# Mixer of a hybrid streaming encoder layer: gate row products ahead of the small root on GpSimd, statistics and shift ahead of taps on VectorE, attention's high parts first on ScalarE

## The reference

```
mod = silu(c) @ w_ada + b_ada;  sh1, sc1, g1, sh2, sc2, g2 = split(mod, 6)
h = x * (1 + sc1) + sh1
proj = h @ w_in                       # q 512 | k 128 | v 128 | a 512 | g 512
attn = window attention of q, k, v with a relative bias and sinks
u    = a * sigmoid(g)
y    = depthwise_conv(u, w_dw, 31 taps) + b_dw
conv = silu(layer_norm(y, cln_g, cln_b))
mix  = concat(attn, conv) @ w_out
x1   = layer_norm(ALPHA * x + (1 + g1) * mix, ln1_g, ln1_b)
h2   = x1 * (1 + sc2) + sh2           # input of router and experts
```

## Time and profile before

| | |
|---|---|
| median of 3 runs | 1524.95 us (1524.7 to 1525.16) |
| profiled execution, its own time | 1525.59 us |
| its span | 1523.8 us |
| busy in the span: PE / DVE / ACT / POOL | 1287.2 / 1265.0 / 823.0 / 681.5 us |
| share of the span | 84% / 83% / 54% / 45% |
| mixer | about 80 to 880 us of the span |

### The profile page before, as it was taken

How to read it: one execution, slowest core, us unless ns; L and a number is a source line. 1 busy time by engine, 2 the same in 40 slices (tenths; PEclk the granted TensorE clock), 3 DMA queues, 4 the chain that set the end, 5 groups by cost and what they waited for, 6 DMA issues and landing times. The chain is left out here.

```text
span 1523.8 us, 25356 instructions
## 1 busy us (share of the span) xinstructions
PE 1287.2 (84%) x7959; PEld 709.3 (47%) x7959; DVE 1265.0 (83%) x3123; ACT 823.0 (54%) x1446; POOL 681.5 (45%) x514
## 2 busy tenths in 40 slices
PE   4588799999999999999995637999999999996665
PEld 3455455555555555555553323444444444443221
DVE  2526799999999999999999477999999999994698
ACT  2413244445554444445554206888888888884122
POOL 0112246767767666776755322222222222220786
PEclk9688899999999999999997958999999999998799
DMA  9964432111111011111111195668993554222896
GB/s 315 299 217 154 148 125 70 44 55 56 56 57 56 32 44 51 48 50 56 43 47 42 55 310 184 241 223 308 338 383 143 193 193 151 110 110 83 205 259 204
DMA packets 106687, 219.38 MB, mean 144 GB/s; under 512 B 11796, under 2 KB 71000, under 8 KB 104547
## 3 DMA queue, kind: packets, MB, share of 16 engines
q1 hardware_dynamic: 82662, 141.23, 27.2%
q0 software_dynamic: 11808, 43.00, 10.0%
q10 hardware_dynamic: 12125, 34.01, 5.7%
HBM read 166.68 MB, written 51.56 MB: 143 GB/s over the span
## 5 line engine op out<-in xcount | busy, mean ns | idle before, releaser
L1157 DVE SCALAR_TENSOR_TENSOR y_sum<-uT,w_dw_cols,y_sum 128x128 f32<-128x128 f32 (+1 forms) x1780 | 462.0, 347 | 0.0
L2085 DVE SCALAR_TENSOR_TENSOR w_gate_up_lo<-w_gate_up_ring,w_gate_up_hi 128x2048 f16<-128x2048 f16 x96 | 219.5, 2289 | 34.5 <-ACT w_gate_up_hi L2007 34.4
L2007 ACT ACTIVATE w_gate_up_hi<-w_gate_up_ring 128x2048 f16 x96 | 182.7, 1905 | 52.4 <-issue 51.3
L1393 PE MATMUL bank<-w_in_hi,hT_hi 128*128 128x512 f16 (+3 forms) x544 | 195.1, 359 | 0.9 <-DVE hT_lo L1295 0.9
L1988 POOL COPY slot_index<-slot_token 128x1 int32 (+1 forms) x48 | 56.4, 1175 | 309.1 <-PE eturn L2149 304.7
L1393 PE MATMUL bank<-w_in_lo,hT_hi 128*128 128x512 f16 (+3 forms) x544 | 194.6, 358 | 0.0
L1393 PE MATMUL bank<-w_in_hi,hT_lo 128*128 128x512 f16 (+3 forms) x544 | 194.4, 357 | 0.0
L2128 PE MATMUL ps_up<-w_gate_up_hi,slot_rowsT_hi 128*128 128x512 f16 x384 | 147.0, 383 | 25.9 <-DVE slot_rowsT_lo L2110 25.7
L2128 PE MATMUL ps_up<-w_gate_up_lo,slot_rowsT_hi 128*128 128x512 f16 x384 | 146.6, 382 | 0.0
L2128 PE MATMUL ps_up<-w_gate_up_hi,slot_rowsT_lo 128*128 128x512 f16 x384 | 146.4, 381 | 0.0
L2116 DVE SCALAR_TENSOR_TENSOR w_down_lo<-w_down_ring,w_down_hi 128x2048 f16<-128x2048 f16 x48 | 109.7, 2285 | 4.0 <-ACT w_down_hi L2061 3.7
(11 more groups left out here) (298 smaller groups left out, 2856.1 us busy)
## 6 DMA issues: line engine op xcount, KB each, us to landing
expert_rows<-out_rows ACTq DMA_DIRECT2D x48, 512.0 KB, 2.8
late<-in_w_ada SPq DMA_DIRECT2D x22, 1024.0 KB, 7.6
w_gate_up_ring<-in_w_gate SPq DMA_DIRECT2D x16, 1024.0 KB, 8.2
w_gate_up_ring<-in_w_up SPq DMA_DIRECT2D x16, 1024.0 KB, 10.9
w_down_ring<-in_w_down SPq DMA_DIRECT2D x16, 1024.0 KB, 12.6
x_h<-in_x_prompt SPq DMA_DIRECT2D x16, 512.0 KB
x_res<-in_x_prompt SPq DMA_DIRECT2D x16, 512.0 KB, 3.6
hidden<-late SPq DMA_DIRECT2D x16, 512.0 KB, 2.6
```

Of the source, the lines that this page charges most:

```text
L1157: dve.scalar_tensor_tensor(total, u, w, y_sum[:, c, :n], ALU.mult, ALU.add).then_inc(taps_done, 1)
L1393: mm = pe.matmul(out, x[xp][:, k, :n], w[wp][:, k, cols], start=(k == 0 and wp == xp), stop=(k == KD - 1 and xp == 1))
L2007: act.activation(gate_up_parts[0][:, at, k:k + KD // 2, :, :].rearrange("p k a n -> p (k a n)"), w_gate_up[:, bass.ds(b, 1), k:k + KD // 2 ...
L2085: dve.scalar_tensor_tensor(flat[1], w_gate_up[:, bass.ds(b, 1), k, :, :].rearrange("p b k a n -> p (b k a n)"), W_SCALE, flat[0], ALU.mult ...
```

## The change

Three edits in `mix`, with the same instructions before and after (1028 rows of program on VectorE, 569 on ScalarE, 416 on GpSimd, in both):

- GpSimd: the two gate products (L877) go into `gate_rows`, called ahead of the y root and of the wait for the residual rows; for tile 15 (`is_next_last`) they stay behind them.
- ScalarE: the high part of attention (L1015) goes ahead of the y normalisation (L1007).
- VectorE: the two taps `cuts[0]` to `cuts[1]` ahead of the residual statistics go behind them: one of them between statistics and shift, in the place of the tap `cuts[1]` to `cuts[2]`, the rest behind the shift and ahead of conv.

```diff
@@ GpSimd, step(i)
                         taps(j)
+                    halves = [slice(h * 512, (h + 1) * 512) for h in range(2)]
+
+                    def gate_rows(j):
+                        n = rows_of(j)
+                        if is_tile(j, 0):
+                            pool.wait_ge(gate_row_loaded, 16)
+                        for h, cols in enumerate(halves):
+                            pool.wait_ge(out_copied, count(2, j, h + 1))
+                            pool.tensor_tensor(v1[:n, cols], v1[:n, cols], rows[:n, 2, cols], ALU.mult).then_inc(gated, 1)
+
+                    if (j := lagged(i, 3)) is not None and not is_next_last(j) and not is_last(j):
+                        gate_rows(j)
                     if (j := lagged(i, 2)) is not None:
...
                         pool.wait_ge(res_loaded, count(16, j, 16))
-                        halves = [slice(h * 512, (h + 1) * 512) for h in range(2)]
-                        if is_tile(j, 0):
-                            pool.wait_ge(gate_row_loaded, 16)
+                        if is_next_last(j):
+                            gate_rows(j)
                         if is_last(j):
                             halves = []
-                        for h, cols in enumerate(halves):
-                            pool.wait_ge(out_copied, count(2, j, h + 1))
-                            pool.tensor_tensor(v1[:n, cols], v1[:n, cols], rows[:n, 2, cols], ALU.mult).then_inc(gated, 1)
@@ ScalarE, step(i)
+                    if (j := lagged(i, 2)) is not None:
+                        n = rows_of(j)
+                        act.wait_ge(pv_done, count(4, j, 4))
+                        if not is_tile(j, 0):
+                            act.wait_ge(out_done, count(2, j))
+                        act.copy(mixT[0][:, 0:4, :n], values_in(n)).then_inc(oT_hi_ready, 1)
                     if (j := lagged(i, 2)) is not None:
...
                         act.activation(y_tok[:n, :].rearrange("p (c q) -> p c q", c=CB), turn_bank("y", 0)[:n, :, :], ACT.Identity,
                                        scale=y_small[:n, 1:2], bias=y_small[:n, 2:3]).then_inc(y_normed, 1)
-                    if (j := lagged(i, 2)) is not None:
...
-                        act.copy(mixT[0][:, 0:4, :n], values_in(n)).then_inc(oT_hi_ready, 1)
@@ VectorE, step(i)
                         score_round(1)
-                    if j1 is not None:
-                        taps(j1, cuts[0], cuts[1])
                     if j3 is not None:
...
                     if j1 is not None:
-                        taps(j1, cuts[1], cuts[2])
+                        taps(j1, cuts[0], cuts[0] + 1)
                     if j3 is not None:
...
+                    if j1 is not None:
+                        taps(j1, cuts[0] + 1, cuts[1])
+                    if j1 is not None:
+                        taps(j1, cuts[1], cuts[2])
                     if j2 is not None:
```

## The result

| | before | changed |
|---|---|---|
| median (4 runs each) | 1524.83 us | 1500.24 us (1497.71 to 1504.27) |
| ratio, 95% interval | | 0.9842 (0.9818 to 0.9865) |
| profiled execution, own time / span | 1525.59 / 1523.8 us | 1498.89 / 1497.2 us |
| busy PE / DVE / ACT / POOL in the span | 1287.2 / 1265.0 / 823.0 / 681.5 us | 1282.3 / 1264.3 / 823.2 / 681.6 us |

24.6 us faster. A second set of runs of the changed kernel gave 1499.72 against 1526.75, ratio 0.9833 (0.9817 to 0.985).

A forecast was written before the change was run, and what follows sets the result against it. The loop through h2, with TensorE waiting for GpSimd's L900, was taken to bound the step. Profiled 1525.59 us minus 22.2 plus 0.3 for step 17 gave 1503.7, or 1503.1 for the median; range 1501 to 1511.

The forecast's parts named there:

- The loop through h2: Turn of x, first taps, both statistics, n1, h2, TensorE to the next turn of x: shortening it shortens the 42.71 us step.
- Part 1: ScalarE copies attention's high parts before the y normalisation, which keeps its time; VectorE from L1226 on comes 1.32 us earlier.
- Parts 2 and 3: VectorE's residual statistics at 472.25 instead of 475.64; GpSimd's early gate products let additions end 2.46 us earlier, root 0.7 to spare.
- n1 held by the kv copy, TensorE the new bound: ScalarE's n1 starts 2.0 us earlier, not 3.4, behind kv; h2 has 0.4 us to spare, so TensorE bounds the step.
- the whole 1.63 goes: TensorE's wait before the turn of h2, 1.63 us in step 9, vanishes entirely.
- 41.08 us a step: Forecast step length with TensorE as the bound, from 42.71 us.
- The term 22.2 us: TensorE's waits before the turn of h2 over fourteen steps (3 to 16), released by GpSimd's L900, counted as gain.
- L1224 stays at 0.96: VectorE's one-column operation keeps its 0.96 us median, since a GpSimd addition replaces the product there; no gain counted.
- Conv before GpSimd in steps 3 to 16, after it in step 17: Conv leads L898 by 0.7 us in steps 3 to 16; in step 17 it is second and held, costing 0.3 us.
- The race: Rival: conv starts after GpSimd's L898 in every step, 0.86 us later each, +12 us, 1537; chance 0.06.
- Half a gain: Rival: a margin overrun by 0.5 to 0.8 us a step leaves 11 to 15 us, 1510 to 1514; chance 0.15.
- no effect: Rival: step closes through VectorE alone, or early products hold up the root by over 0.7 us; 1525, chance 0.05.

The follow-up runs named there:

- the gate rows alone: The kernel before with only GpSimd's edit, the gate products ahead of the y root: 1527.73 against 1527.99 us, ratio 1.0001.
- high parts back: The changed kernel with ScalarE's attention high part behind the y normalisation again: 1551.72 us, ratio 1.0162 to the kernel before.
- conv first: The changed kernel with attention's high part behind the y normalisation again and conv directly behind the residual shift: 1516.02 us, ratio 0.9929 to the kernel before.
- one tap later: The changed kernel with one tap (four operations, 1.05 us) moved from behind conv to ahead of it: 1516.54 us, ratio 0.9937 to the kernel before.
- the gate rows back: The changed kernel with GpSimd's gate row products behind the y root again: 1553.76 us, ratio 1.0177 to the kernel before.

## Why the prediction was right or wrong

**The loop through h2 binds the step.** Right. Delaying the shift by three taps made h2 late again and lengthened the step by 1.50 us, and the gate rows alone, which release nothing that VectorE waits for, changed nothing.

**Part 1** (1.32 us off VectorE, y normalisation unmoved). Right: no wait before mixT_lo, and alone it gives 1.10 us a step. Here too the wait was worth a little more than the bracket: from the y statistics to mixT_lo it was 472.15 - 467.75 = 4.40 us and is 457.83 - 454.83 = 3.00, so 1.40 and not 1.32. The missing 0.08 is the overlap that neighbouring VectorE rows show where none waits.

**Parts 2 and 3** (statistics 3.39 us earlier, root 0.7 us to spare). Right: the statistics start at 459.24, 4.41 us behind the y statistics at 454.83, where 4.5 was forecast, and the root had 0.72.

**n1 held by the kv copy, TensorE the new bound.** Right: n1 starts right behind kv, and giving TensorE less idle time shortened the step further (40.71, 40.40). hT_lo's wait came out at 0.97 where 1.03 was forecast, in part by luck: VectorE gained more than 1.32 us and the step shortened by more than 1.63, and the two errors nearly cancel.

**The size of the wait, "the whole 1.63 goes", "41.08 us a step".** This step failed: the stall was priced at its bracket, 1.63 us, and cost 1.86. The term 22.2 us is the sum of idle times between the modelled end of one matmul and the start of the next, and a stall costs more. The last matmuls of the g projection and the turn of h2, before and after:

```profile
482.53 0.38 PE L1393 MATMUL bank<-w_in_lo,hT_hi 128*128 128x512 f16 x1
482.75 0.38 PE L1393 MATMUL bank<-w_in_hi,hT_lo 128*128 128x512 f16 x1
```

```profile
469.62 0.38 PE L1403 MATMUL bank<-w_in_lo,hT_hi 128*128 128x512 f16 x1
469.83 0.38 PE L1403 MATMUL bank<-w_in_hi,hT_lo 128*128 128x512 f16 x1
```

Each is shown 0.38 us long, but the next starts 0.22 after it starts. After the change the turn starts at 470.05, 0.22 behind 469.83. Before, it started at 484.76, 2.01 behind 482.75. The stall took 1.79 us from start to start, 0.16 more than the bracket says, and the turn itself is 1.09 instead of 1.04 us long. The Trainium skill, "TensorE: Matmul & The Clock Gate", section "Step-by-step: what each phase is for", gives a mechanism: the fill of a matmul hides the drain of the one before, and a matmul by itself can't hide its drain. The trace agrees so far: 0.38 us for one, 0.22 from start to start, and the difference is the 0.16. No run here isolates the drain, so that this is the cause is not shown; the size of the loss is.

The whole term can be read from the steps too. From the h2 turn of step 3 to that of step 16 it was 783.71 - 228.89 = 554.82 us and is 756.02 - 225.18 = 530.84: 24.0 us less, where the thirteen brackets add up to 21.2. (The profiled executions are 26.7 us apart, but 2.6 of that lie ahead of the y statistics of step 2 and do not come from the change.) The term should have been 22.2 + 14 x 0.22 = 25.3 us. With it the sum reads 1525.59 - 25.3 + 0.3 = 1500.6, and 1500.0 for the median; 1500.24 was measured. That the two agree to 0.3 us is luck, with executions of this kernel 6.6 us apart.

**L1224 stays at 0.96.** Right. It is L1232 in the changed kernel, and its group over the span, against the earlier trace rows, reads

```profile
L1232 DVE SCALAR_TENSOR_TENSOR small<-small x16: 152/958/965, 163.1 to 781.8; 128x1 f32<-128x1 f32 x15, 64x1 f32<-64x1 f32 x1
```

A median of 0.958 us behind an addition, where it was 0.960 behind a product.

**Conv before GpSimd in steps 3 to 16, after it in step 17.** Right in both, to 0.03 us (0.76 against 0.74, 2.26 against 2.27). Four runs show the lock from the other side: conv is 0.7 us long when it starts first and 2.3 to 2.6 when it starts second, whether VectorE's 1.32 us wait is there (high parts back against conv first) or not (one tap later). The one exception is the race at 0.09 us in step 4 of the run with one tap later. The cost of step 17 was +0.57 us (79.34 us from h2 turn to h2 turn in the kernel before, 79.91 after) and not +0.3: the h2 turn came earlier into a TensorE that then stood 2.88 us for the probabilities, and their eight turns took 1.97 us instead of 1.45, at a lower granted clock (0.82 from 793 to 836 us, where it was 0.91 from 824 to 863). How much of the 0.57 each of these makes is not shown: with the gate rows alone the same distance is 80.57 us (781.50 to 862.07), with TensorE's waits for h2 and the probabilities as before, but 1.97 us for those turns and a granted clock of 0.78 (822 to 862). So the lower clock can make this step over 1 us longer.

**The rivals.** The race was real: conv starts 0.75 to 0.76 us first in steps 5 to 16, 1.27 and 0.96 us first in steps 3 and 4, and leaving out ScalarE's or GpSimd's edit brings it about (1551.7 and 1553.8 us). "1537" underrated it for two reasons: in the first run five long steps at a lower clock add 10.3 us, and in the second, where the clock stays at 1.00, VectorE comes to conv 2.3 us later and the step is 44.37 us instead of the 43.57 that the rival's sum gives. Half a gain and no effect did not occur.

**The range** had a low end of 1501.4 from step 17 alone, and took the wait's size as certain. That is where it was too narrow.

What stays open: why the preparation differs by up to 2.7 us between executions, why the clock falls in some steps and not in others with the same waits, and what makes up the last 0.01 to 0.02 us of a stall's cost. None was tried.

## What to carry to other kernels

Value a wait of TensorE by starts, not by the idle time in the bracket: the distance from the last matmul's start to the next one's, less the distance they have back to back. Here that adds 0.16 us to each stall, and the turn behind it is 0.05 us longer: 0.22 us in all at the four lengths that were measured. Before moving work in time on VectorE or GpSimd, list the VectorE operations with two SBUF operands and GpSimd's long operations and see which comes first: a tap's worth of 1 us in the wrong place cost 1.5 us a step, and the three edits without ScalarE's or without GpSimd's are slower than none, while without VectorE's they are still faster (1507.95 us).

## What the runs showed of the hardware that was not expected

- A stall of TensorE between fp16 products and an fp32 turn costs 0.22 us beyond its shown idle time, at 0.23, 0.54, 1.27 and 1.63 us shown.
- A VectorE operation held by GpSimd lengthens the GpSimd operation that follows at once: L908 is 2.69 us long beside a held conv and 2.36 otherwise. That conv runs in between the two is the likely reading (it ends 0.54 us behind the first), not shown.
- The hold can fall on GpSimd too. It was seen once: in a close race (0.09 us apart) conv kept its 0.68 us, and GpSimd's L906 took 2.99 us instead of 2.36.
- Short waits of TensorE in succession (0.84 and 1.40 us in a step) went with a granted clock of 0.94 over two steps, with steps 1.4 to 2.5 us longer than their neighbours of the same order, in some steps and not in others. In the run with the gate rows back TensorE waited as long at the same places, and the granted clock stayed at 1.00.
